# The two widest blocks of a top-256 search: compared on GpSimd and added up on ScalarE instead of counted on VectorE

## The reference, cut to what matters

```python
dots = jnp.einsum('bqhd,bkd->bqhk', qi, ki, preferred_element_type=F32)
score = jnp.einsum('bqhk,bqh->bqk', jax.nn.relu(dots), wi.astype(F32))
adm = (k_pos[None, :] // CHUNK) <= (q_pos[:, None] // CHUNK)
score = jnp.where(adm[None], score, NEG_INF)
_, idx = lax.top_k(score, topk)          # topk = 256
...
kg = jax.vmap(lambda t, ii: t[ii])(k, idx)
vg = jax.vmap(lambda t, ii: t[ii])(v, idx)
```

## Time and profile before

| | |
|---|---|
| median of 3 runs | 3683.62 us (3671.93 to 3686.56) |
| the profiled execution | 3671.88 us, of which the span from first to last instruction is 3670.1 us |
| mean granted TensorE clock | 0.924 of full speed |
| TensorE matmuls busy | 3181.3 us (87% of the span) |
| VectorE busy | 1624.7 us (44%) |
| ScalarE busy | 900.7 us (25%) |
| GpSimd busy | 460.0 us (13%) |

### The profile page before, as it was taken

The page is one execution under the profiler, slowest core; times in us unless marked ns, Lnnn a source line. Parts: engine busy times, 40 slices in busy tenths (PEclk is TensorE's granted clock), DMA queues, the critical chain, the costliest instruction groups (busy, mean ns, idle before and its releaser), DMA issues. The chain is left out here.

```text
span 3670.1 us, 48632 instructions
## 1 busy us (share of the span) xinstructions
PE 3181.3 (87%) x17386; PEld 2632.6 (72%) x17386; DVE 1624.7 (44%) x3146; ACT 900.7 (25%) x1885; POOL 460.0 (13%) x589
## 2 busy tenths in 40 slices
PE   4699799999896999999995997039787899999997
PEld 0244365376686999999984767027576899999996
DVE  0000255464335534444443489953235453534354
ACT  0000143333315202121213320036423320202022
POOL 0000011011002111111101000026411111111110
PEclk8799978999898999999997999569899999999999
DMA  7533300000101111111102001010120111111111
GB/s 209 164 125 140 113 1 18 1 1 7 35 23 35 43 49 46 41 52 40 46 30 76 29 18 44 0 46 1 36 93 12 46 40 52 43 49 42 51 37 59
DMA packets 48157, 182.75 MB, mean 50 GB/s; under 512 B 5289, under 2 KB 11977, under 8 KB 40809
## 3 DMA queue, kind: packets, MB, share of 16 engines
q1 hardware_dynamic: 44480, 171.14, 13.9%
q10 hardware_dynamic: 3528, 9.64, 1.5%
HBM read 163.31 MB, written 17.45 MB: 49 GB/s over the span
## 5 line engine op out<-in xcount | busy, mean ns | idle before, releaser
L549 PE MATMUL ps<-t_hh,t_wh 128*128 128x352 f32 x2112 | 683.7, 324 | 66.8 <-DVE t_wlo L638 66.8
L549 PE MATMUL ps<-t_hl,t_wh 128*128 128x352 f32 x2112 | 679.1, 322 | 0.0
L549 PE MATMUL ps<-t_hh,t_wlo 128*128 128x352 f32 x2112 | 678.6, 321 | 0.0
L638 DVE TENSOR_TENSOR t_wlo<-t_wraw,t_wh 128x1024 fp32r<-128x1024 f32 (+2 forms) x152 | 164.7, 1085 | 793.2 <-POOL t_wh L526 792.6
L549 PEld LDWEIGHTS ps<-t_hh,t_wh 128*128 128x128 f32 x2112 | 398.0, 188 | 68.0 <-DVE t_wlo L638 68.0
L549 PEld LDWEIGHTS ps<-t_hl,t_wh 128*128 128x128 f32 x2112 | 398.6, 189 | 0.0
L549 PEld LDWEIGHTS ps<-t_hh,t_wlo 128*128 128x128 f32 x2112 | 397.7, 188 | 0.0
L618 ACT ACTIVATE t_u<-ps 128x352 f32<-128x352 f32 (+1 forms) x352 | 124.2, 390 | 948.5 <-PE ps L549 887.2
L549 PE MATMUL ps<-t_sh,t_wh 128*128 128x352 f32 x1056 | 341.3, 323 | 2.2 <-DVE t_xT L709 1.7
L549 PE MATMUL ps<-t_sl,t_wh 128*128 128x352 f32 x1056 | 340.8, 323 | 0.0
L549 PE MATMUL ps<-t_sh,t_wlo 128*128 128x352 f32 x1056 | 340.8, 323 | 0.0
(11 more groups left out here) (250 smaller groups left out, 5128.0 us busy)
## 6 DMA issues: line engine op xcount, KB each, us to landing
t_wada<-in_wada SPq DMA_DIRECT2D x48, 1024.0 KB, 4.8
t_wraw<-in_wfi SPq DMA_DIRECT2D x88, 512.0 KB, 3.6
t_wraw<-in_wfo SPq DMA_DIRECT2D x32, 384.0 KB, 3.1
t_wraw<-in_wfo SPq DMA_DIRECT2D x32, 320.0 KB, 2.9
t_wo_raw<-in_wo SPq DMA_DIRECT2D x15, 512.0 KB, 3.7
rel_scratch<-t_kpe ACTq DMA_DIRECT2D x1, 5124.0 KB
t_xT<-in_xT SPq DMA_DIRECT2D x1, 4224.0 KB, 13.1
x_scratch<-t_xT SPq DMA_DIRECT2D x1, 4224.0 KB, 18.4
```

Of the source, the lines that this page charges most:

```text
L549: mm = nc.tensor.matmul(ps[:, bank, 0:NT], w[:, b, k], x[:, slots[k], cols], start=k == n == 0, stop=k == total - 1 and n == 2)
L638: nc.vector.tensor_tensor(wlo[:, b, 0:k], raw[:, b, 0:k], wh[:, b, 0:k].bitcast(F32), ALU.subtract) \
```

## The change

The seven blocks are put in three groups instead of two: three blocks (384, 512, 640 keys), two (768, 896) and two (1024, 1056). The last two are no longer counted by VectorE. GpSimd compares their scores with the level and writes flags (bf16) into one of two buffers in the idle half of the relu scratch; ScalarE copies the flags in place with an accumulator, which gives the count. VectorE still does all small operations, now for three groups. In a step it issues those of group 1 and of group 2 (the new one) behind the counts of group 0, and those of group 0 behind the two counts of group 1. `kept` of group 2 waits for ScalarE's semaphore `added`; GpSimd's compare of the next step waits for `narrowed`. The casts of tiles 7 to 14 follow the compares of steps 3, 5, ..., 17 in GpSimd's queue, the low parts come at the end of VectorE's steps 4, 6, ..., 18, and ScalarE moves tiles 5 to 14 out behind its sums of steps 1, 3, ..., 19. Masks are made as before.

```diff
-        self.cut = n // 2
...
+        ends = ((0, 3), (3, 5), (5, n))
+        self.groups = [sels[x:y] for x, y in ends]
+        self.cols = [slice(x, y) for x, y in ends]
+
+
+STEPS = 32
+CAST_STEP = 3
...
+        flags = [relu[0].bitcast(BF16)[:, u * N:(u + 1) * N] for u in range(2)]
...
             @block.gpsimd
             def _(pool):
-                for i in range(ODD_TILES):
+                def cast(i):
                     pool.wait_ge(loaded[i % 2], 16 * (i // 2 + 1))
                     if i >= 2:
                         pool.wait_ge(S["ready"], NTOK * (i - 1))
                     nc.gpsimd.tensor_copy(wh[:, i % 2], raw[:, i % 2]).then_inc(S["w_hi"], 1)
+
+                def compare(step):
+                    for u, s in enumerate(find.groups[2]):
+                        if step == 0:
+                            pool.wait_ge(S["scored"], 1)
+                        else:
+                            pool.wait_ge(S["narrowed"], 3 * step)
+                            pool.wait_ge(S["added"], 2 * (step - 1) + u + 1)
+                        level = find.level[s.rows, s.col:s.col + 1].bitcast(F32) if step else 0.0
+                        nc.gpsimd.tensor_scalar(flags[u][s.rows, 0:s.kb.nk], s.score[s.rows], level, None, ALU.is_ge) \
+                            .then_inc(S["compared"], 1)
+
+                late = INDEX_TILES + 2
+                for i in range(late):
+                    cast(i)
+                for step in range(STEPS):
+                    compare(step)
+                    if step >= CAST_STEP and (step - CAST_STEP) % 2 == 0 and late < ODD_TILES:
+                        cast(late)
+                        late += 1
...
-                for i in range(ODD_TILES):
-                    if i == INDEX_TILES:
-                        index_relu()
+                def add(step):
+                    for u, s in enumerate(find.groups[2]):
+                        act.wait_ge(S["compared"], 2 * step + u + 1)
+                        if step:
+                            act.wait_ge(S["narrowed"], 3 * step)
+                        f = flags[u][s.rows, 0:s.kb.nk]
+                        nc.scalar.activation(f, f, ACT.Copy, accum_out=find.count[s.rows, s.col:s.col + 1]) \
+                            .then_inc(S["added"], 1)
+
+                for i in range(INDEX_TILES):
                     tile(i)
+                index_relu()
+                late = INDEX_TILES
+                for step in range(STEPS):
+                    add(step)
+                    if step % 2 and late < ODD_TILES:
+                        tile(late)
+                        late += 1
+                assert late == ODD_TILES
...
-                def narrow(g, bit, counted):
+                def narrow(g, bit, counted, signal):
...
-                    dve.wait_ge(S["counted"], counted)
+                    dve.wait_ge(signal, counted)
...
-                    n, due, late = 0, iter(()), INDEX_TILES + 2
+                    n, late = 0, INDEX_TILES + 2
+                    second = third = iter(())
                     for bit in range(31, -1, -1):
-                        for g, group in enumerate(find.groups):
-                            if bit < 31:
-                                dve.wait_ge(S["narrowed"], 2 * (31 - bit) - 1 + g)
+                        step = 31 - bit
+                        first = iter(())
+                        for g, group in enumerate(find.groups[:2]):
+                            if step:
+                                dve.wait_ge(S["narrowed"], 3 * (step - 1) + (1, 3)[g])
                             for s in group:
-                                at_least(s, level_of(s) if bit < 31 else 0.0, n)
+                                at_least(s, level_of(s) if step else 0.0, n)
                                 n += 1
-                                next(due, None)
-                            for _ in due:
+                                next(first if g else second, None)
+                                if g == 0:
+                                    next(third, None)
+                            for _ in first if g else second:
                                 pass
-                            due = narrow(g, bit, n)
-                        if bit % 2 == 0 and late < ODD_TILES:
+                            for _ in third if g == 0 else ():
+                                pass
+                            if g == 0:
+                                first = narrow(0, bit, n, S["counted"])
+                        second = narrow(1, bit, n, S["counted"])
+                        third = narrow(2, bit, 2 * (step + 1), S["added"])
+                        if step >= CAST_STEP + 1 and (step - CAST_STEP) % 2 and late < ODD_TILES:
                             low(late)
                             late += 1
...
-                chain.wait()
+                dve.wait_ge(S["summed"], len(sels) * HEADS)
+                chain.wait(S["scored"])
                 masks(search())
```

More of the change, by code:

```diff
@@ L1705, in __init__ @@
         self.count = m.sb("sel_count", [P, n], ctx)
-        self.groups = [sels[:self.cut], sels[self.cut:]]
-        self.cols = [slice(0, self.cut), slice(self.cut, n)]
+        ends = ((0, 3), (3, 5), (5, n))
[3 more added lines that the diff above has]
+CAST_STEP = 3
 def odd_tiles(m, hh, hl, qd, kd, ki, qi, v, wi, sels, spare):
@@ L1718, in odd_tiles @@
         S = {n: m.sem("o_" + n) for n in ("w_hi", "w_lo", "ready", "moved", "c_loaded", "out", "x_saved",
-                                          "i_ready", "i_moved", "summed", "chain", "counted", "narrowed")}
+                                          "i_ready", "i_moved", "summed", "chain", "counted", "narrowed", "scored", "compared", "added")}
         loaded = [m.sem(f"wo_loaded{u}") for u in range(2)]
@@ L1886, in search @@
                 def search():
-                    n, due, late = 0, iter(()), INDEX_TILES + 2
+                    n, late = 0, INDEX_TILES + 2
+                    second = third = iter(())
                     for bit in range(31, -1, -1):
-                        for g, group in enumerate(find.groups):
-                            if bit < 31:
-                                dve.wait_ge(S["narrowed"], 2 * (31 - bit) - 1 + g)
+                        step = 31 - bit
[3 more added lines that the diff above has]
+                                dve.wait_ge(S["narrowed"], 3 * (step - 1) + (1, 3)[g])
                             for s in group:
-                                at_least(s, level_of(s) if bit < 31 else 0.0, n)
+                                at_least(s, level_of(s) if step else 0.0, n)
                                 n += 1
-                                next(due, None)
-                            for _ in due:
-                                pass
-                            due = narrow(g, bit, n)
-                        if bit % 2 == 0 and late < ODD_TILES:
+                                next(first if g else second, None)
+                                if g == 0:
+                                    next(third, None)
+                            for _ in first if g else second:
+                                pass
+                            for _ in third if g == 0 else ():
[5 more added lines that the diff above has]
+                        if step >= CAST_STEP + 1 and (step - CAST_STEP) % 2 and late < ODD_TILES:
                             low(late)
                             late += 1
-                    for _ in due:
-                        pass
-                    dve.wait_ge(S["narrowed"], 64)
+                    for rest in (second, third):
+                        for _ in rest:
+                            pass
+                    dve.wait_ge(S["narrowed"], 3 * STEPS)
                     return n
```

## The result

The changed kernel took 3731.93 us (median of 4 runs, 3731.63 to 3733.09), the kernel before 3677.77 (4 runs, 3669.18 to 3686.56): a ratio of 1.0148, 95% interval 1.0119 to 1.0177. It is slower, and outside the range that I gave. Rival 3 is what happened.

What follows compares the result with a forecast made beforehand. A loop of GpSimd, ScalarE and VectorE was taken to bound the search: 129 + 65 C, 207 us at C = 1.2, 29 less; profiled 3671.9 becomes 3643, plus 11.7 for the median: 3655 us, forecast range 3640 to 3668, 8-in-10 range 3640 to 3708.

Steps and rivals of the forecast that it cites:

- Rival 3: In GpSimd's compare: it costs about the addition's 2.37 us, search 283 us, time 3731 us, slower; chance 0.25.
- C: Time of one GpSimd compare of 1024 columns, taken as 1.2 us; the 1056-column one as 1.03 times that.
- The bound above: Upper end of the range for GpSimd's compare: 2.37 us, the price of an addition with two inputs.
- The loop bounds the search: In each search step the loop GpSimd, ScalarE, VectorE, not VectorE's own 5.2 us, sets the time if C exceeds 0.84.
- 3.5 + 2.03 C: Length in us of one search step: 3.5 for VectorE, ScalarE's sum and wake-ups, 2.03 C for both GpSimd compares.
- the formula: Whole search: 32 x (3.5 + 2.03 C) + 15 + 2 = 129 + 65 C us, 207 at C = 1.2.
- That single number decides: GpSimd's compare time, expected about 1.2 us in 64 rows, decides between the forecast, a dearer compare without difference, and Rival 3.
- The sign changes at C = 1.65: For the whole kernel: faster below this compare time, slower above; measurably faster below 1.37, measurably slower above 1.93.
- The port costs nothing beyond what was counted: On the port shared by GpSimd and VectorE: held small operations fall into VectorE's 2.4 us wait, so no extra cost.
- Rival 2: GpSimd keeps the shared port over both compares: 0.65 us more a step, gain 8 us, time 3676 us; chance 0.07.
- Casts and splits: In the search: eight casts holding the port 1.04 us and eight splits of 1.13, 17.4 us, of which 15 taken.
- TensorE ends at 2284 as before: TensorE's last tile in the search ends near 2284 us, as before (2283), hidden by 70 us of search.

Runs made afterwards that it cites:

- the list of forms: Changed kernel with GpSimd doing eight forms in turn (compares, subtract, multiply, copies, compare and multiply) at the 1024 block; ran once, 3730.14 us.
- the spread tiles: Against the two-loop Sign version: ScalarE moves one third of a projection tile out per step, splits every third step; 3628.80 us, 0.9855 of the kernel before.

## Why the prediction was wrong

The step that failed is the size of one term, C. "A compare against one value per partition reads one tensor, as the cast does; I take 1.2". It measured 2.84 us. I had sorted GpSimd's prices by the number of inputs, and the list of forms shows that with one input they go by whether anything is computed. The bound above, the addition's 2.37 us, was too low as well: an operation with one input and a scalar is dearer than one with two inputs. The trace before had no row of a scalar operation on GpSimd of this size, and 2.37 was the nearest row, but no reason made it the upper end.

The Trainium skill (GPSIMD Engine Reference, section 4.1) calls one-input work "roughly line-rate". That agrees with the copies, 1.04 us, and not with the compare, the multiplication or the subtraction. Its 1.8 cycles an element (section 3.1), an estimated 1.54 us, is also below the 2.84 measured. The measurement decides.

Point by point:
- **The loop bounds the search: right.** The prediction had 3.5 + 2.03 C a step. Measured: 3.37 + 5.77, and with the copy 3.37 + 2.05. At the copy's price the formula gives 129 + 65 x 1.04 = 197 us; the kernel with the copy has 198.3. What makes these agree is partly luck: 16 us of its search lie in four steps in which ScalarE is held by tiles, for which the formula had 2 us, and casts and splits cost less than its 15.
- **"That single number decides": shown**, by the copy in its place with every wait left (0.9904). The halved width (0.9922) points the same way.
- **The sign changes at C = 1.65: not tried at that point.** The half-wide compares, 1.57 us, were faster than before, but they also halve the add-up.
- **The port costs nothing beyond what was counted: right in the cost, not in the picture.** The prediction had `kept` of group 0 stretched until the compare ends. It took 0.26 us instead of 0.17 and was over 1.7 us before that end (last section). `kept` of group 1 takes 0.94 us, right ahead of the 3.03 us in which VectorE waits for the sum anyway. Rival 2, one more hold of 0.65 a step, would have been seen in the 3.37 and is not there.
- **Casts and splits: 15 us predicted, about 5 measured.** A cast runs in the 3.4 us in which GpSimd waits for the level, and a split in VectorE's wait for the sum. What a split does cost is the compares beside it:

```profile
2180.72 6.41 POOL L1771 TENSOR_SCALAR t_xT<-t_xT,t_sel_level 128x1024 bf16<-128x1024 f32 x2 [2.39 <-DVE t_sel_level L1918]
2190.51 5.77 POOL L1771 TENSOR_SCALAR t_xT<-t_xT,t_sel_level 128x1024 bf16<-128x1024 f32 x2 [3.38 <-DVE t_sel_level L1918]
2196.24 1.03 POOL L1761 CAST t_wo_hi<-t_wo_raw 128x1024 fp32r<-128x1024 f32 x1
...
2183.09 1.22 DVE L1871 TENSOR_TENSOR t_wo_lo<-t_wo_raw,t_wo_hi 128x1024 fp32r<-128x1024 f32 x1
```

  6.41 instead of 5.77, eight times: 5.2 us. With the shorter loop I had no such cover to count on, and for the long one I should have worked the term out anew.
- **TensorE ends at 2284 as before: wrong**, by 47 us, and without effect.
- **Rival 3, 3731 us: right in its mechanism and its place.** That its time came out to the microsecond is chance. It took C = 2.37 and a search of 283 us, and added the 11.7 us by which the median before lay above the profiled execution. The search is 296.4 us, 13 more, and nothing has to be added: the changed kernel's profiled time, 3731.8, is within 0.2 of its median. The two errors cancel. At C = 2.84 the prediction's formula, with the measured pair, gives 32 x (3.5 + 5.77) + 17 = 314, 17 us too much, most of it for casts and splits.

What stays open: why arithmetic on GpSimd costs 2.5 ns per column. It isn't the number of partitions: the compare of 32 x 1056 took 2.95 us, the one of 128 x 1024 2.84.

## What to carry to other kernels

Before work moves to GpSimd, its price has to come from a row of the same operation there; a copy or a cast of the same tile says nothing about arithmetic, which here took 2.7 times as long. Where the result of a step sets the next step, the price of the helpers counts in full as latency, so work out the whole loop of engines and split it into loops that run beside each other (9.14 to 6.18 us a step here, with the same compares and add-ups). And look for one instruction on one engine in place of two on two: Sign with an accumulator on ScalarE does in 1.15 us what the pair did in 2.84 and 1.06, and together with the spread tiles and a third block it turned 1.5% slower into 1.8% faster.

## What the runs showed of the hardware

- **Scalar arithmetic on GpSimd**, f32 in, takes 2.77 to 2.85 us for 1024 columns in the three operations tried (is_ge, subtract, mult), with bf16 or f32 out, the scalar a constant or from a tile; the compare takes 2.50 ns per column and 0.28 us fixed; a second operation in the instruction adds 0.87; copies and casts take 1.04.
- **A slow compare does not hold VectorE for its whole length.** In the step shown above the compare ran from 2350.50 to about 2353.3. `kept` of group 0 started at 2351.38, took 0.26 and was over at 2351.64, 1.14 us after the compare's start, and `prefix`, with two inputs, took its usual 0.15 at 2352.62. The second compare held a `kept` that started at 2353.54 until 2354.48, which is about 1.1 us after its start too. With half the columns the hold ends earlier (timelines of GpSimd and VectorE):

```profile
2341.09 3.13 POOL L1772 TENSOR_SCALAR t_xT<-t_xT,t_sel_level 128x512 bf16<-128x512 f32 x2 [2.93 <-DVE t_sel_level L1919]
...
2341.97 0.16 DVE L1906 TENSOR_SCALAR t_sel_kept<-t_sel_count 128x3 int32<-128x3 f32 x1
...
2343.11 0.23 DVE L1915 TENSOR_TENSOR t_sel_prefix<-t_sel_prefix,t_sel_kept 128x3 int32<-128x3 int32 x1
```

  `kept` is not held at all, 0.88 us after the first compare's start, and `prefix` is over 0.71 us after the start of the second, at about 2342.63. So the hold goes with the width; at 1024 columns it lasts about as long as a copy of the tile (1.04 us), and not as long as the compare. The casts of the earlier trace rows held VectorE to their end, but they last only 1.04. The Trainium skill (SBUF — State Buffer, section "SBUF: two separate sides") tells of a lock for the whole instruction; the casts agree with it and these compares do not. Why the hold ends there no run shows.
- **The other way round, VectorE holds up GpSimd:** in the step with the split shown above, the first compare takes its usual 2.85 us and the second 3.58 instead of 2.94. It starts while the split of two inputs is running (2183.09 to 2184.31), and is lengthened by about what was left of it. The split itself takes 1.22, about its usual time.
